# Two experts as an interleaved pair in place of one expert after the other

## The reference

```
logits = (x @ w_router) + b_router
top_v, top_i = lax.top_k(logits, 2)
combine = sum(one_hot(top_i, 8) * softmax(top_v), axis=-2)
for e in range(8):
    out = out + combine[..., e:e + 1] * swiglu(x, wg[e], wu[e], wd[e])
```

## Time and profile before

| | us |
|---|---|
| median of 3 runs (lowest to highest) | 1430.02 (1429.59 to 1430.86) |
| the profiled execution, its own time | 1430.79 |
| its span, first to last instruction | 1428.8 |
| PE busy | 1317.5 (92% of the span) |
| PE weight loads busy | 1084.5 (76%) |
| DVE busy | 1142.5 (80%) |
| ACT busy | 938.6 (66%) |
| POOL busy | 124.2 (9%) |

### The profile page before, as it was taken

How to read it: one execution, slowest core, us unless ns; L and a number is a source line. 1 busy time by engine, 2 the same in 40 slices (tenths; PEclk the granted TensorE clock), 3 DMA queues, 4 the chain that set the end, 5 groups by cost and what they waited for, 6 DMA issues and landing times.

```text
span 1428.8 us, 18212 instructions
## 1 busy us (share of the span) xinstructions
PE 1317.5 (92%) x6740; PEld 1084.5 (76%) x6740; DVE 1142.5 (80%) x959; ACT 938.6 (66%) x743; POOL 124.2 (9%) x126
## 2 busy tenths in 40 slices
PE   7998999989998999988999998999998899999885
PEld 7898999979887788656788765678875577886663
DVE  6776554467576998898889789988879988988997
ACT  5543534445434776888777688867778886777885
POOL 3433000023522000000000000000000000000001
PEclk9999999999996999999999999999999999999998
DMA  9634555634435997998999799899899989979990
GB/s 330 221 122 167 176 196 186 193 130 166 159 118 192 347 355 289 399 409 334 387 409 374 282 409 398 317 404 402 294 366 391 391 319 410 388 275 398 409 358 31
DMA packets 133183, 425.12 MB, mean 298 GB/s; under 512 B 9280, under 2 KB 11616, under 8 KB 133104
## 3 DMA queue, kind: packets, MB, share of 16 engines
q1 hardware_dynamic: 131456, 419.17, 78.3%
q0 software_dynamic: 1504, 4.76, 1.1%
q10 hardware_dynamic: 144, 0.07, 0.0%
HBM read 422.92 MB, written 1.05 MB: 297 GB/s over the span
## 4 chain that ended last, share of the span: by engine, by line
PE 67%; DVE 15%; ACT 8%; issue 8%; DMA 1%; SPq 0%; ACTq 0%; DVEq 0%
PE bank L1456 17%; PE bank L1458 17%; PE bank L1457 17%; DVE w_lo L946 9%; ACT w_hi L667 6%; PE bank L1756 4%; PE bank L1757 4%; PE bank L1728 2%; PE bank L1752 2%; DVE arena L1018 1%; PE bank L1821 1%; DVE arena L1361 1%; DMA raw<-in_w_in 1%; ACT arena L852 1%; PE bank L1593 1%
## 5 line engine op out<-in xcount | busy, mean ns | idle before, releaser
L946 DVE TENSOR_TENSOR w_lo<-raw,w_hi 128x2048 fp32r<-128x2048 f32 x303 | 692.6, 2299 | 202.0 <-ACT w_hi L667 200.6
L667 ACT CAST w_hi<-raw 128x2048 fp32r<-128x2048 f32 x303 | 575.0, 1910 | 232.4 <-PE bank L1458 205.9
L1456 PE MATMUL bank<-w_hi,parts 128*128 128x512 f32 x824 | 332.0, 403 | 4.6 <-DVE w_lo L946 2.4
L1756 PE MATMUL bank<-w_hi,parts 128*128 128x512 f32 x672 | 281.6, 419 | 55.7 <-DVE w_lo L946 54.3
L1458 PE MATMUL bank<-w_hi,parts 128*128 128x512 f32 x824 | 322.1, 391 | 0.0
L1457 PE MATMUL bank<-w_lo,parts 128*128 128x512 f32 x824 | 321.8, 391 | 0.0
L1757 PE MATMUL bank<-w_lo,parts 128*128 128x512 f32 x672 | 264.5, 394 | 0.0
L1756 PEld LDWEIGHTS bank<-w_hi,parts 128*128 128x128 f32 x672 | 126.6, 188 | 121.2 <-DVE w_lo L946 86.9
L1456 PEld LDWEIGHTS bank<-w_hi,parts 128*128 128x128 f32 x824 | 155.2, 188 | 44.2 <-DVE w_lo L946 8.0
L1457 PEld LDWEIGHTS bank<-w_lo,parts 128*128 128x128 f32 x824 | 155.3, 188 | 33.1 <-issue 2.9
L1458 PEld LDWEIGHTS bank<-w_hi,parts 128*128 128x128 f32 x824 | 155.0, 188 | 33.3
(11 more groups left out here) (226 smaller groups left out, 1033.2 us busy)
## 6 DMA issues: line engine op xcount, KB each, us to landing
raw<-in_wg_exp SPq DMA_DIRECT2D x96, 1024.0 KB, 7.4
raw<-in_wd_exp SPq DMA_DIRECT2D x96, 1024.0 KB, 7.8
raw<-in_wu_exp SPq DMA_DIRECT2D x48, 1024.0 KB, 8.0
arena<-in_wu_exp SPq DMA_DIRECT2D x48, 1024.0 KB, 8.8
raw<-in_w_in SPq DMA_DIRECT2D x20, 1024.0 KB, 6.8
tokens<-in_wu_exp SPq DMA_DIRECT2D x16, 1024.0 KB, 8.1
raw<-in_wg_dense SPq DMA_DIRECT2D x11, 1024.0 KB, 5.1
raw<-in_wu_dense SPq DMA_DIRECT2D x11, 1024.0 KB, 5.1
```

The costliest lines, as they stand in the source:

```text
L667: a.copy(w_hi[:, n % SPLIT, :], slot(n)).then_inc(hi_ready, 1)
L946: v.tensor_tensor(w_lo[:, n % SPLIT, :], slot(n), w_hi[:, n % SPLIT, :].bitcast(F32), ALU.subtract).then_inc(lo_ready, 1)
L1456: mm(psum, left[0], right[0], start=first, stop=False)
L1756: mm(psum, left, right[0], start=first, stop=False)
```

## The change

Four pairs of a wide item (stream A) and a narrow one (stream B) take the place of eight items. Within a pair the two streams alternate in blocks of four units (two in the last block): A gate, B gate, A up, B up, A down, B down. The 84 units of a pair begin with block 0's gate and up units and then the down units of the pair before that were left over, those of its last block ("late"). In the first pair, A gate is followed at once by A up.

- A sums gate and up one after the other in banks 2 and 3, where its transposes go too (`WORK_A`); B in banks 6 and 7 (`WORK_B`). Output sums are in 0 and 1 (A) and 4 and 5 (B). The product of silu and up is written over `esg` and `esg_n`. So an up block waits for silu of the same banks, and the next gate block for the low parts.
- The fold of B comes two units after the block that it belongs to ended, within A's units.
- The two outputs of a pair (`y_a`, `y_b`) are scattered together: two products into one sum for each of four quarters, and one addition for each by DVE, into four different banks. All eight products stand behind the third and the fourth of A's gate units of block 1.
- The order of the experts is worked out by DVE ahead of the first units (`item_order`), since the second stream needs an expert that isn't known beforehand. The weights of the combination move behind it. The other tables follow in the first pair. PE counts the tokens of each expert (two small products) before DVE takes the positions.
- The ring's slots come from a table: nine in turn for 36 units, then eight for 48, so that a slot comes round after eight or nine units everywhere.
- The gathers of the next pair's tokens stand at units 74, 77 and 79. The last pair gathers nothing.

In the diff `done(p, v)` is the value of `unit_done` or `lo_ready` once unit v of pair p is through; `LATE` is 4, `ROUND` is 20.

```diff
-PAIRS = E // 2 - 1
+PAIRS = E // 2
...
-TURN = {10: 0, 20: 1, 32: 2, 38: 3}
-SCATTER = {2: 0, 4: 1, 6: 2, 8: 3}
-STEP_SLOTS, STEP_PICK = 16, 20
-GATHER = {33: 0, 38: 1}
-TAKE = {36: 0, 40: 1}
+def pair_order():
+
+    out = []
+    for b in range(EXP_BLOCKS):
+        before = (b - 1) % EXP_BLOCKS
+        for stream, kind, blk in (("A", "g", b), ("B", "g", b), ("A", "u", b), ("B", "u", b), ("A", "d", before),
+                                  ("B", "d", before)):
+            out += [(stream, kind, blk, q) for q in range(block_units(blk))]
+    return out
...
+        self.fold_g = {(v if first and b == 0 else v + 2): b for v, b in self.gate_b.items()}
+        self.fold_u = {v + 2: b for v, b in self.up_b.items()}
+        self.turn_a = {(v + 4 if b < EXP_BLOCKS - 1 else v + 3): b for v, b in self.up_a.items()}
+        self.turn_b = {(v + 4 if first and b == 0 else v + 5): b for v, b in self.up_b.items()}
...
+LATE_A, LATE_B = ROUND - LATE // 2 - 1, ROUND - 1
+SCATTER = {ROUND + 2: (0, 1), ROUND + 3: (2, 3)}
+ADD = {ROUND + 4: 0, ROUND + 5: 1, ROUND + 6: 2, ROUND + 7: 3}
+STEP_CUR, STEP_SLOTS_A, STEP_SLOTS_B, STEP_PICK_A, STEP_PICK_B = 46, 47, 48, 54, 57
+STEP_SLOTS = 68
+GATHER_A = {74: 0, 77: 1}
+GATHER_B, GATHER_B_FIRST = 79, 9
...
+RING = 9
+SLOT = [s for n in (9, 9, 9, 9, 8, 8, 8, 8, 8, 8) for s in range(n)]
...
+            def round_unit(s, h, landed_at, free):
+                act.wait_ge(*landed_at)
+                act.wait_ge(unit_done, free)
+                a.copy(w_hi[:, h, :], ring[s]).then_inc(hi_ready, 1)
...
+                    round_unit(SLOT[v], v % SPLIT, landing(p, v), done(p, v - SPLIT))
...
+                    if v in at.gate_a:
+                        b = at.gate_a[v]
+                        act.wait_ge(unit_done, done(p, v))
+                        if b or not first:
+                            act.wait_ge(eturn_a, p * FILLS + (turned_fills(b - 1) if b else 0))
+                        gate_silu(b, esg, WORK_A, P)
...
+                    if v in at.fold_g:
+                        b = at.fold_g[v]
+                        act.wait_ge(fold_mm, 2 * EXP_BLOCKS * p + (2 * b + 1))
+                        if b or not first:
+                            act.wait_ge(eturn_b, EXP_BLOCKS * p + b)
+                        gate_silu(b, esg_n, WORK_B, NARROW)
...
+            def item_order():
+
+                v.tensor_copy(count, bank[0][:, 4 * E:5 * E]).then_inc(count_ready, 1)
+                dve.wait_ge(count_ready, 1)
+                st.then(v.tensor_tensor(key, count, cst[:, C_BIG:C_BIG + E], ALU.add))
...
+                st.then(v.tensor_tensor(above, sel, each(cst[:, C_CE:C_CE + E], E), ALU.mult))
+                st.then(v.tensor_reduce(order_f, above, AX_X, ALU.add))
+                v.tensor_copy(order_int[:, 2:E + 2], order_f).then_inc(order_ready, 1)
...
+                mm(psum, scat[:, 0, at_t], y_a[:, at_d], start=True, stop=False)
+                mm(psum, scat[:, 1, at_t], y_b[:, at_d], start=False, stop=True).then_inc(scattered, 1)
```

More of the change, by code:

```diff
@@ L513, in _, with fetch @@
                 load(mixer_unit(1, kind, half), mixer_source(1, kind, half))
[L515 to L519 removed]
+            def fetch(s, src, landed_at):
+                n = src.shape[2]
+                sp.dma_start(ring[s].rearrange("p (k n) -> p k n", n=n), src).then_inc(landed_at[0], 16)
@@ new lines, in pair_loads @@
+            def pair_loads(p, order, experts, first=False):
+                for v, unit in enumerate(order):
+                    if unit is None:
+                        continue
+                    stream, kind, b, q = unit
+                    before = [w for w in uses(SLOT[v]) if w < v and order[w] is not None]
+                    if before:
+                        sp.wait_ge(lo_ready, done(p, before[-1]))
+                    elif not first:
+                        sp.wait_ge(lo_ready, done(p - 1, uses(SLOT[v])[-1]))
+                    elif v - LATE < RAW:
+                        sp.wait_ge(lo_ready, MOE_UNIT0 + v - LATE - RAW + 1)
+                    elif SLOT[v] == 1:
+                        sp.wait_ge(ylo_ready, 4 * LAYERS)
+                    elif SLOT[v] == 2:
+                        sp.wait_ge(logit_mm, 1)
+                    else:
+                        sp.wait_ge(tokens_free, 1)
+                    fetch(SLOT[v], expert_source(kind, b, q, experts(stream, kind, b, v)), landing(p, v))
@@ new lines, in take_a, with take_b, gate_silu @@
+            def take_a(i, n):
+                act.wait_ge(gather_a, 2 * i + (n - 1))
+                a.copy(four(xg_lo, n), bank[GATHER_BANKS[1]])
+                a.copy(four(xg_hi, n), bank[GATHER_BANKS[0]]).then_inc(xg_ready, 1)
+            def take_b(i, banks):
+                for n in range(2):
+                    act.wait_ge(gather_b, 2 * i + (n + 1))
+                    a.copy(four(xg_n, n), bank[banks[n]]).then_inc(xgn_ready, 1)
+            def gate_silu(b, to, n, rows):
+                w = EXP_WIDTH[b]
+                a.activation(to[0:rows, 0:w], wide_bank(n, w, rows), ACT.Silu).then_inc(esilu, 1)
@@ L930, in _ @@
                     with act.If(j < n_over):
-                        wide_item(j + E, True)
+                        extra(j)
             for t in range(TT):
@@ new lines, in hidden_low_b, with pair @@
+            def hidden_low_b(i, b):
+                n = EXP_WIDTH[b] // P
+                dve.wait_ge(ehi_b, i * EXP_BLOCKS + (b + 1))
+                v.tensor_tensor(eh_n[:, 0:n, NARROW:],
+                                bank[WORK_B][:, 0:n * NARROW].rearrange("p (j c) -> p j c", c=NARROW),
+                                eh_n[:, 0:n, 0:NARROW].bitcast(F32), ALU.subtract).then_inc(elo_b, 1)
+            def pair(p, first=False, last=False):
+                at = IN_FIRST if first else IN_PAIR
+                for u in range(LATE if first else 0, PAIR_UNITS):
+                    if u > LATE or not first:
+                        subtract_expert(p, u + AHEAD)
```

911 lines of the change are left out of this document (517 added, 394 removed).

## The result

The changed kernel takes 1447.35 us (median of four runs, 1443.45 to 1451.74), the kernel before 1430.44 in the same session (1429.59 to 1431.08): the ratio is 1.0121, 95% interval 1.0097 to 1.0145. The forecast was 1438, 8 us slower; it came out 17 us slower. The side and the range hold, the size doesn't.

The account below looks back on a forecast made before the run. PE was taken to bound wide items, the weight split with two units of lead narrow ones, DMA hidden. Start 454.8, pairs 232.2, 2 x 242.3 and 235.4, late units 9.3, then the tail, gave 1438 us; range 1384 to 1458.

Parts of the forecast that it names:

- the layout: Expert pairs: 24 units laid out on three engines take 64.2 us; a pair 242.3, against 238.6 to 240 before.
- round 1 with the scatters: Block 1 of a pair: all eight scatter products stand in A blocks, plus 7.3 us, 71.5 in all.
- round 2 with the picks: Second full round of a pair: picks and slots add 1.6 us to the 64.2 of a round.
- last round: Pair's last 16 units: gather halves, slots and a silu wait make 50.2 us where 42.8 are pro rata.
- last pair: Fourth pair of experts: it has no gathers, so 235.4 us against 242.3 for a middle pair.
- first pair: 80 units, no scatters or adds, but waits for silu, table load and fold: 232.2 us.
- The routing cost: Before the first expert unit: working out the order adds 2.2 us, so the first unit starts at 454.8.
- the pieces of the earlier trace: Durations used for all expert blocks, such as 0.23 us a matmul; the method was trusted to some 2%.
- 1, that the blocks even out: Expert pairs: DVE never stops, a pair takes 215 to 226 us, total 1340 to 1385; chance 0.17.
- the rule on regimes: Expert phase: interleaving regimes with different most-contended engines may help; a pair goes towards the larger of the engines' sums.
- 2, DMA: Narrow items: DMA was the bound; closing the transfer hole saves some 6 us an item, 48 in all, 1382; chance 0.08.
- 3, that ACT's queue reaches into the A blocks: A blocks: a chain 0.7 to 1 us longer makes PE wait there too, 25 us more, 1463; chance 0.14.

Follow-up runs that it names:

- e8: Changed kernel plus six zero-matrix matmuls after the second unit of every B block of four: 1451.58 us.
- e9: Changed kernel with ACT's two sum copies at a pair's start placed three and two units later: 1448.15 us, ratio 1.0108.
- e13: Changed kernel with the narrow gathers of the later pairs left out, all but two matmuls in each passage: 1439.3 us.
- e14: Changed kernel with the wide gathers of the later pairs left out, all but four matmuls in each passage: 1438.63 us.
- e3: Changed kernel with four split slots instead of three, paid for with four raw buffers in the earlier parts and a seven-slot ring: 1377.99 us, ratio 0.9633.
- e5: Kernel before, own item order, with four split slots, four raw buffers in the earlier parts and a seven-slot ring: 1392.96 us, ratio 0.9732.
- e7: Kernel before with only four raw buffers in the earlier parts and a seven-slot ring, three split slots kept: 1427.42 us, ratio 0.9965.
- e4: Changed kernel with only four raw buffers in the earlier parts and a seven-slot ring, three split slots kept: 1448.97 us, ratio 1.0119.
- e6: Changed kernel with blocks of two, scatters and narrow gather in B blocks, four split slots, fewer raw buffers and a seven-slot ring: 1360.92 us, ratio 0.9518.
- e2: Changed kernel with A and B alternating in blocks of two units, scatters and narrow gather in B blocks, three split slots: 1463.39 us, ratio 1.0219.
- e1: Changed kernel with the scatter products and the narrow gather moved from A blocks into B blocks: 1435.59 us.

## Why the forecast had the side right and the size wrong

**Right: the layout.** PE's timeline of the changed kernel, first units of the pair, of round 1, round 2 and the last round, and of the next pair:

```profile
686.28 0.50 PE L1647 MATMUL bank<-w_hi,parts 128*128 128x512 f32 x1
...
741.18 0.50 PE L1647 MATMUL bank<-w_hi,parts 128*128 128x512 f32 x1 [2.20 <-DVE w_lo L1105]
...
812.46 0.50 PE L1647 MATMUL bank<-w_hi,parts 128*128 128x512 f32 x1
...
877.51 0.50 PE L1647 MATMUL bank<-w_hi,parts 128*128 128x512 f32 x1
...
1126.84 0.50 PE L1647 MATMUL bank<-w_hi,parts 128*128 128x512 f32 x1
...
1177.07 0.47 PE L1647 MATMUL bank<-w_hi,parts 128*128 128x512 f32 x1 [0.18 <-DVE w_lo L1105]
```

| term | forecast | trace |
|---|---|---|
| first 20 units of a pair | 54.8 | 54.9 |
| round 1 with the scatters | 71.5 | 71.3 |
| round 2 with the picks | 65.8 | 65.1 |
| last round | 50.2 | 50.2 (second), 53.7 (first, partly at 1.2 GHz) |
| last pair | 235.4 | 235.4 (1.5 of it from 1.2 GHz) |
| late units | 9.3 | 9.5 |
| first pair | 232.2 | 234.0 (2.3 of it from 1.2 GHz) |
| first unit | 454.8 | 452.2 |
| last sum copy to the span's end | 20.7 | 19.7 |

The routing cost what was said: from the last logits to the first unit it takes 16.1 us instead of 13.9; the part ahead of it ran 2.6 us earlier in this execution.

**Wrong, the failed step: "the pieces of the earlier trace rows" were taken at one clock everywhere, and the loop turn wasn't a term.** Laid out at the earlier trace rows's 0.23 us a matmul, the sum had no term for the stretches in which TensorE runs at 1.2 GHz instead of 2.4. In the changed kernel they are here (windows, columns as above, the granted clock third from the end):

```profile
916.00:920.00 4.00, 4.00 (x26) 3.81 (x26) 1.46 (x2) 1.55 (x3) 0.00 (x0) 0.72 0.90 326
920.00:924.00 4.00, 4.00 (x13) 2.75 (x12) 2.29 (x1) 2.81 (x2) 0.00 (x0) 0.50 0.51 193
...
988.00:992.00 4.00, 3.03 (x8) 2.40 (x9) 3.98 (x3) 3.10 (x3) 0.00 (x0) 0.68 0.97 351
992.00:996.00 4.00, 4.00 (x21) 3.03 (x21) 2.12 (x2) 1.74 (x2) 0.00 (x0) 0.90 1.02 366
```

The first costs 3.5 us (the last round of 53.7 against 50.2), the second 1.6 (the A block with the scatters takes 19.98 us against 18.40 at 741), a third at 1232 1.5. The first pair starts so too (clock 0.50 up to 454, 0.63 from there to 458): its first 11 matmuls take 4.8 us, 2.3 more than at 0.23 each. That makes 8.9 us, and the loop turn costs 2.9. Up to B's last sum copy (1421.96) the trace stands 5.7 us above the forecast: -2.6 for the start, +1.8 for the first pair, +2.6 and +3.6 for the middle pairs, 0 for the last, +0.2 for the late units. Without the lower clock and the loop turn the pairs are 231.7, 241.4, 241.4 and 233.9, where 232.2, 242.3, 242.3 and 235.4 were forecast. So the missing terms came to 11.8 us, and an earlier start and pairs laid out a little too long hid half of them; that the last pair agrees to 0.1 us is luck.

The remaining 4 us lie between this execution (1443.45, mean clock 0.973) and the median (1447.35). Over the four runs of the changed kernel time goes with the mean granted clock, 1.1 us for each 0.001; over 55 runs of the kernel before it is 1.0. Their mean clocks are 0.969 and 0.974, so of the 17 us 4 to 5 go with the mean clock. The other 12 to 13 are the difference of the two profiled executions (1443.45 and 1430.79), whose means are alike (0.973 and 0.974). But a mean over the program counts stretches in which PE has little to do: the kernel before is at 0.72 from 1410 to 1428, with PE busy for 5.2 us of the 18. In the expert phase it loses only some 3 us to the lower clock, at its first matmuls and at 1058 to 1066, where the changed kernel loses 8.9. An estimate from these rows: 4 us by the mean clock, 6 by where the lower clock falls, and 7 for the order itself with its loop turn, where the forecast had 8 in all.

What brings the lower clock is **not settled**. Filling part of PE's waits in B blocks didn't lift it (e8), nor did moving the sum copies (e9) or leaving out one gather or the other (e13, e14). Nor does the stop of 2.2 us ahead of round 1 bring it each time: it stands at 741.18, 988.97 and 1231.84, and only the last two have the lower clock behind them. The profiled execution of every kernel of the changed order (blocks of four) with three slots has a stretch of it between 916 and 944; where it falls otherwise varies from kernel to kernel.

**The rivals.** 1, that the blocks even out, is right about what interleaving can do and wrong about this kernel: what it describes came with the third unit of lead that e3 gave, 225 to 228 us for a middle pair, at the upper end of its 215 to 226. By the rule on regimes (the Trainium skill, Perfetto Trace Analysis, Optimization Strategy) the order may pay: with three units of lead the runs agree, 15 us (e3 against e5), with two they don't, -17. 2, DMA, gave 5 us in e7, none of it in the first narrow item, and nothing in e4. The rule that HBM is nearly always the bottleneck (the Trainium skill, SBUF — State Buffer, A bandwidth-pool intuition that's wrong) isn't borne out here: the changed kernel's pairs move 355 to 365 GB/s where 410 is reached in the earlier trace rows, and nothing waits for a transfer. It comes closer as the lead grows, with 402 GB/s and waits of ACT for transfers in e6. 3, that ACT's queue reaches into the A blocks, didn't come in blocks of four (the three A blocks of round 2 take 11.0 to 11.5 us) and did come in e2. No row shows how large the slack there was. In e2 it was the rival that its expectation names, a pair over 238 and a total over 1430; a good part of that chain is on DVE, not only in ACT's queue.

## What to carry to other kernels

Before reordering work to even out two regimes, work out the chain around the split buffer: release by the consumer, each preparing step, the signals, plus each small step queued on the same engines. It must be shorter than the consumer's work on the units in between, at every place of the new order. If it isn't, a deeper buffer comes first: here the order alone lost 17 us, the fourth slot alone gained 34 (e5 against e7, which have the same ring), and the two together, in blocks of two and with the scatters moved, 72.

A forecast made of block lengths can be good to 1 us in a middle pair of 245 and still miss by half a per cent, if it takes the engine's clock and loop turns for free.

## What the runs showed of the hardware

- Time follows the mean granted TensorE clock within one program: in e1 ten runs go from 1427.42 at 0.977 to 1441.57 at 0.966. A difference of 10 us between two kernels of this length needs the clock beside it.
- A loop turn on PE, ACT, DVE and SP together cost 2.9 us in the block behind it, with 1.64 of issue on PE and a gap of 5.2 us in ACT; written out, two pairs of code cost nothing visible.
- 216 matmuls put into PE's waits were all but free (4 us for 50 us of work, e8) and didn't lift its granted clock (0.966 to 0.969, where the changed kernel has 0.965 to 0.973).
- Closing a hole in the transfers (202 GB/s before, 404 to 407 in e7) didn't shorten the item around it (113.0 us in both) while nothing waited for a transfer.
